# A two-layer transformer kernel: the score and mask matmuls of the stick-breaking attention, ordered by head instead of by query tile

## The reference

```python
def stick_breaking_attention(q, k, v):           # 16 heads of 64
    strict = key_pos[None, :] < q_pos[:, None]
    z = einsum('bthd,bshd->bhts', qb, k) * (HEAD_DIM ** -0.5)
    brk = where(strict, softplus(z), 0.0)
    remain = cumsum(later(brk), reverse=True)
    a = where(strict, exp(log_sigmoid(z) - remain), 0.0)
    return einsum('bhts,bshd->bthd', a, v)
```

## Time and profile before

| | us |
|---|---|
| median of 3 runs | 1029.02 |
| lowest and highest run | 1026.81, 1029.56 |
| the profiled execution: its own time | 1026.81 |
| the profiled execution: its span | 1025.0 |
| TensorE busy in the span | 1008.9 (98%) |
| VectorE, ScalarE busy | 573.5 (56%), 477.0 (47%) |

### The profile page before, as it was taken

How to read it: one execution, slowest core, us unless ns; L and a number is a source line. 1 busy time by engine, 2 the same in 40 slices (tenths; PEclk the granted TensorE clock), 3 DMA queues, 4 the chain that set the end, 5 groups by cost and what they waited for, 6 DMA issues and landing times.

```text
span 1025.0 us, 12715 instructions
## 1 busy us (share of the span) xinstructions
PE 1008.9 (98%) x4774; PEld 824.6 (80%) x4774; DVE 573.5 (56%) x624; ACT 477.0 (47%) x522; POOL 33.6 (3%) x63
## 2 busy tenths in 40 slices
PE   6999999999999999999999999999999999999998
PEld 5767888888888878888888888777888888888887
DVE  4675754454573756754544485664456774545453
ACT  5545634444355654644343455445534454444432
POOL 1020100000000000000000022000000000000000
DMA  8731756555555333555555555334444356555641
GB/s 261 265 121 44 246 176 205 168 200 180 189 184 195 135 123 123 196 195 188 180 199 173 201 186 185 114 129 148 164 164 164 139 190 218 192 186 182 199 170 41
DMA packets 113590, 177.31 MB, mean 173 GB/s; under 512 B 7696, under 2 KB 75920, under 8 KB 113552
## 3 DMA queue, kind: packets, MB, share of 16 engines
q1 hardware_dynamic: 112400, 172.80, 49.8%
q0 software_dynamic: 864, 3.41, 1.0%
q10 hardware_dynamic: 288, 0.59, 0.2%
HBM read 175.72 MB, written 1.05 MB: 172 GB/s over the span
## 4 chain that ended last, share of the span: by engine, by line
PE 93%; DVE 3%; DMA 1%; POOL 1%; SPq 1%; issue 0%; ACT 0%; ACTq 0%; DVEq 0%
PE psum L1293 28%; PE psum L1295 27%; PE psum L1294 27%; PE psum L1350 4%; PE psum L1370 2%; DVE low L896 1%; PE psum L1372 1%; DMA raw<-in_ev_w_in 1%; DVE arena L1090 1%; PE psum L1576 1%; DMA cst<-consts 1%; DVE small L1089 1%; PE psum L1390 1%; PE psum L1599 1%; POOL head_rs L531 0%; SPq L470 0%
## 5 line engine op out<-in xcount | busy, mean ns | idle before, releaser
L896 DVE TENSOR_TENSOR low<-raw,high 128x2048 fp32r<-128x2048 f32 (+1 forms) x163 | 369.6, 2268 | 307.1 <-ACT high L570 306.8
L570 ACT ACTIVATE high<-raw 128x2048 fp32r<-128x2048 f32 (+1 forms) x163 | 308.9, 1895 | 256.5 <-PE psum L1295 250.9
L1293 PE MATMUL psum<-high,xh 128*128 128x512 f32 x912 | 362.4, 397 | 0.0
L1295 PE MATMUL psum<-high,xl 128*128 128x512 f32 x912 | 356.0, 390 | 0.0
L1294 PE MATMUL psum<-low,xh 128*128 128x512 f32 x912 | 355.3, 390 | 0.0
L1295 PEld LDWEIGHTS psum<-high,xl 128*128 128x128 f32 x912 | 171.2, 188 | 36.7
L1293 PEld LDWEIGHTS psum<-high,xh 128*128 128x128 f32 x912 | 171.3, 188 | 35.0 <-issue 2.0
L1294 PEld LDWEIGHTS psum<-low,xh 128*128 128x128 f32 x912 | 171.5, 188 | 33.4
L1293 PE MATMUL psum<-high,gh 128*128 128x512 f32 x240 | 93.6, 390 | 0.0
L1295 PE MATMUL psum<-high,gl 128*128 128x512 f32 x240 | 93.4, 389 | 0.0
L1294 PE MATMUL psum<-low,gh 128*128 128x512 f32 x240 | 93.4, 389 | 0.0
(11 more groups left out here) (144 smaller groups left out, 656.7 us busy)
## 6 DMA issues: line engine op xcount, KB each, us to landing
raw<-in_ffn_w SPq DMA_DIRECT2D x132, 512.0 KB, 4.3
raw<-in_w_in SPq DMA_DIRECT2D x52, 512.0 KB, 4.4
raw<-in_od_w_qkv SPq DMA_DIRECT2D x24, 512.0 KB, 4.6
raw<-in_w_ffn_gate SPq DMA_DIRECT2D x22, 512.0 KB, 3.7
raw<-in_w_ffn_up SPq DMA_DIRECT2D x22, 512.0 KB, 4.7
raw<-in_w_ffn_down SPq DMA_DIRECT2D x22, 512.0 KB, 4.0
raw<-in_ev_w_in SPq DMA_DIRECT2D x12, 512.0 KB, 6.3
raw<-in_ev_w_out SPq DMA_DIRECT2D x8, 512.0 KB, 4.7
```

The costliest lines, as they stand in the source:

```text
L570: nc.scalar.activation(high[:, n % RING, 0:cols], raw[:, n % RING, 0:cols], ACT.Copy).then_inc(high_ready, 1)
L896: nc.vector.tensor_tensor(low[:, n % RING, 0:cols], raw[:, n % RING, 0:cols], high[:, n % RING, 0:cols].bitcast(F32), ALU.subtract).then_i ...
L1293: nc.tensor.matmul(out, sh, wh, start=start, stop=False, skip_group_check=True)
L1295: return nc.tensor.matmul(out, sl, wh, start=False, stop=stop, skip_group_check=True)
```

## The change

In `stick_z` the loop runs over the heads first and over the query tiles inside. The two mask matmuls of 256 columns (one per head, over both diagonal blocks through a strided PSUM view and a broadcast mask) become four of 128 columns, each directly behind the score matmul of its block. Each block is now an accumulation group of its own: score with `start=True`, mask with `stop=True`. Of query tiles, tile 0 (128 columns) now comes before tile 1 (256 columns). Waits and the semaphore signal at the end stay.

```diff
-                for t, (c0, c1) in enumerate(((P, TRI), (0, P))):
-                    for e in range(2):
-                        rows = slice(e * HD, (e + 1) * HD)
-                        q, k = o_qT[rows, half, j, (1 - t) * P:(2 - t) * P], o_kT[rows, half, j, 0:c1 - c0]
-                        nc.tensor.matmul(bank(Z_BANK + e, c0, c1), q, k, start=t == 0, stop=False, skip_group_check=True)
-                mask = strictr[:, :].unsqueeze(1).to_broadcast([P, 2, P])
                 for e in range(2):
-                    diagonal = psum[:, Z_BANK + e, :].rearrange("p (b n) -> p b n", n=P)[:, 0:3:2, :]
-                    ins = nc.tensor.matmul(diagonal, identr[:], mask, start=False, stop=True, skip_group_check=True)
+                    rows = slice(e * HD, (e + 1) * HD)
+                    q, k = o_qT[rows, half, j, :], o_kT[rows, half, j, :]
+                    for t, (c0, c1) in enumerate(((0, P), (P, TRI))):
+                        nc.tensor.matmul(bank(Z_BANK + e, c0, c1), q[:, t * P:(t + 1) * P], k[:, 0:c1 - c0], start=True, stop=False,
+                                         skip_group_check=True)
+                        ins = nc.tensor.matmul(bank(Z_BANK + e, c1 - P, c1), identr[:], strictr[:], start=False, stop=True,
+                                               skip_group_check=True)
                 ins.then_inc(z_ready, 1)
```

## The result

The changed kernel takes 1044.99 us (median of 4 runs, 1044.02 to 1060.37), the kernel before 1029.29 us in the runs beside it. The ratio is 1.0166, 95% interval 1.0137 to 1.0195: slower by 17 us at the middle of the interval, and 15.7 us between the medians. Nine further runs of the changed kernel took 1043.21 to 1050.35 us; the mean of its 12 runs is 1046.1 us against 1029.1 us of the four before, and that is the ratio. (The run of 1060.37 us fell in a disturbed state of the chip; it is in the median of four, and not in the 12 and the ratio.)

A forecast was written before the change was run, and what follows sets the result against it. TensorE was taken to bound the kernel; eight pairs at +1.88 us add 15.0 us, giving 1041.8 us from the profiled execution or 1044.0 from the median. The forecast was 1043.5 us, range 1038.5 to 1047.

The forecast's parts named there:

- The bound: Stage of the eight pairs: TensorE busy 64.00 of 64 us, so its added time appears one to one in the end.
- the microsecond: Sign of being wrong: a stage without the eight blocks changes its length by over a microsecond.
- The price of a pair: Each stick_z block goes from 1.42 to 3.30 us, +1.88: scores +1.22, masks +0.61, next product +0.05.
- the sum that starts from the median: Whole kernel: 15.0 us added to the median of three runs instead of the profiled execution, giving 1044.0 us.
- What was named as the cause: Score blocks: masks between heads end their running side by side; four masks for two; eight switches between 64-row and 128-row matmuls.
- The late product: Line 1153's product before the next transposes, third pair: spare time grows from 1.0 to about 1.7 us, no new wait.
- (a): Rival at the eight blocks: paced only by streamed columns, a pair stays 1.42 us, time 1029.0 us; chance 0.04.
- (b): Rival at the eight blocks: only lost head overlap is paid, +3.6 us, or 8.5 us with masks; chance 0.05.
- lower bound: Scores stream singly at full-array rate, 1.30 - 0.85 = +0.45 us a pair, masks unchanged; 3.6 us in all.
- (c): Rival: full price plus a late product, 1.0 us lost at each of seven transposes, 1051 us; chance 0.03.

The follow-up runs named there:

- the experiment by head: Against the kernel before, the four scores run head by head, with the two 256-column masks whole at the end; 1031.16 against 1029.67 us, ratio 1.0008.
- same rows: Against the kernel before, head 1 of each pair reads head 0's queries and keys in array rows 0 to 63; ratio 1.0027, block 2.07 us.
- masks split: Against the kernel before, only the two 256-column masks become four of 128 columns, in a row at the block's end; 1031.32 against 1029.67 us, ratio 1.0008.
- two places: Against the kernel before, heads still alternate but two 128-column masks stand behind each query tile's scores; ratio 1.0021, block 1.97 us.

## Why the prediction was right

**The bound.** TensorE was to be the bound in the stage and its time to appear one to one. The stage has 14.79 us more, TensorE is busy for all of them, and behind it the span is the same to 0.01 us. Ahead of it the profile was 2.62 us longer, more than the microsecond that the prediction named as a sign of being wrong. The experiments show that this comes and goes with the single execution, in kernels with the same instructions there.

**The price of a pair.** 1.88 us was taken from the third layer's pair, and it is 1.88. Eight of them are 15.0, the stage shows 14.79: of the seven stretches between the pairs, of products and transposes, five came out 0.04 us shorter each. The two comparisons give 15.7 and 15.3 us between the medians.

**The median.** The forecast of 1043.5 is 1.5 us below the 1044.99 measured. Of that, 0.5 lies in setting it below the sum that starts from the median (1044.0). The rest is within what two medians of one kernel differ by here (1029.02 and 1030.81), and with the clocks that the runs happen to get, a forecast can't come nearer than that except by luck.

**What was named as the cause** holds. The prediction said that the heads run beside each other and that the mask between them takes this away, and it named the narrow masks and the further ways between 64-row and 128-row matmuls beside it. What it left open is whether the alternating order matters by itself. It does not: without a mask between them, the heads overlap in either order (1.43 us). In the changed kernel both come together, so the sum did not suffer, but the expectation for the experiment by head took the order for the cause, and was wrong by almost 5 us. The prediction took its price whole from the third layer; the experiments divide the 1.88 us:
- the overlap of the heads by array rows: 0.65 us (same rows against before)
- four narrow masks for two wide ones: 0.22 us (masks split against before)
- what is left, for three further ways into and out of 64-row matmuls: 1.88 - 0.65 - 0.22 = 1.01, which is 0.34 each. By itself one measured 0.33 (two places against one with split masks), and 2.46 - 1.42 - 0.65 = 0.39 where a wide mask stands between the heads.

Each such way is also one between fp32r (products and masks) and fp32 (scores), which no experiment took apart. The retention of the kernel before does: it goes from fp32r products to fp32 matmuls and back with all array rows, and pays nothing. The first fp32 matmul starts at 743.54, and the product ahead of it at 743.31: 0.23 us, the step of products among themselves. At the other end it is 748.95 - 748.28 = 0.67 us from the last fp32 matmul to the second product, 0.43 for the one and 0.23 for the other:

```profile
748.28 0.59 PE L1701 MATMUL psum<-arena 128*128 128x256 f32 x2
...
748.95 0.40 PE L1294 MATMUL psum<-low,xh 128*128 128x512 f32 x1
```

So the price goes with the 64 rows and not with the number format.

The Trainium skill has a rule for each of the two larger parts. "Mode switching requires drain", it says in TensorEngine Tiling (Array Packing), Key Properties. The trace agrees in that a way in and out has a price, 0.33 us; that the time goes into draining, no run shows. The Trainium skill's page TensorE: Matmul & The Clock Gate, Part 3: Packing small matmuls, has matmuls in different row groups running at the same time. The trace agrees: 0.85 us for two heads in different rows against 1.50 in the same.

**The late product.** It was to have about 1.7 us to spare at the third pair. In the changed kernel ScalarE takes the scores 0.20 us after the block, and the product is done 1.57 us before the transposes:

```profile
355.29 0.81 ACT L778 ACTIVATE arena<-psum 128x768 f32<-128x768 f32 x1 [1.14 <-PE psum L1578]
...
358.06 0.96 DVE L1153 TENSOR_TENSOR arena<-arena 128x768 f32<-128x768 f32 x1
...
360.59 0.81 PE L1598 MATMUL psum<-cst,arena 128*128 128x128 f32 x6
```

**The rivals.** (a), paced by columns, would have left the blocks at 1.42 us; the columns are the same and the block is 2.3 times as long. (b) was a part of the cost, not all of it: its 0.45 us for the overlap is 0.65 when measured. The 1.30 us of its lower bound are scores without any going over, while the 0.85 us hold some, 0.20 us, which remains when the overlap is lost (1.50 us in the same rows). (c), a late product, did not come.

## What to carry to other kernels

Where small matmuls of 64 rows meet full-array ones, count the changes between the two kinds, not the columns. Here each way in and out cost 0.33 to 0.39 us, so matmuls of one kind belong together, with one wide mask for two narrow ones. Heads in different array rows overlapped here only while no full-array matmul stood between them. And when a kernel holds the new order already in another place, read the price there, and then look whether that place should have the old order: here it gave some 7 us between runs of equal clock.

## What the runs showed of the hardware

- Two heads of 384 score columns in fp32, one in array rows 0 to 63 and one in 64 to 127, take as long as one: 0.85 us, in both orders. In the same rows they take 1.50 us, and 1.68 us with a full-array matmul between them.
- Matmuls of one half of the rows overtook those of the other: four passes of 256 columns, two of each head, started before any of 128, against the written order.
- One way from full-array matmuls into 64-row ones and out again costs 0.33 to 0.39 us. Going from fp32r to fp32 and back with all rows costs nothing (0.23 us, the step of products among themselves).
- Four 128-column fp32r masks of the full array in a row take 0.50 us; alone between two 64-row matmuls such a mask takes 0.26 us.
- The granted clock can fall in part of the stretch near 78 us (a mean of 0.54 to 0.87 over 76 to 80 us in eight of ten profiles) and stay at 1.00 in another execution of the same kernel (0.64 and 1.00). What decides it was not tried.
